# Recurrent block of a two-layer fp32 kernel: the Gelu branch with tokens on partitions, the first convolution tap on ScalarE, the end of the block in quarters

## Chip, cores, metric

One NeuronCore of a Trainium2 chip runs the whole program. The metric is device time in microseconds (us), the median of several executions. Engines are named as in the profile: PE (TensorE matmul), PEld (its weight load), DVE (VectorE), ACT (ScalarE), POOL (GpSimd), SP (SyncE, which issues the weight transfers).

## The reference, cut to the block that changes

The program computes an attention layer with an MLP, a recurrent layer with an MLP, and then a second network (convolution and linear-attention mixing, then a mixture of experts with gathered rows). Only the recurrent layer's mixer is touched. Its input h is 256 tokens by 1024 features, everything is fp32.

```python
def rglru_block(h, w_in, conv_w, conv_b, w_a, b_a, w_x, b_x, lam, w_o):
    proj = h @ w_in                                   # 1024 -> 2048
    gate = jax.nn.gelu(proj[..., :RG_WIDTH])          # RG_WIDTH = 1024
    xc = causal_depthwise_conv(proj[..., RG_WIDTH:], conv_w, conv_b)   # 4 taps
    xh = xc.reshape(B, S, RG_BLOCKS, RG_BLOCK_DIM)
    r = jax.nn.sigmoid(einsum('bshi,hij->bshj', xh, w_a) + b_a)
    i = jax.nn.sigmoid(einsum('bshi,hij->bshj', xh, w_x) + b_x)
    log_a = (-RG_C * r) * jax.nn.softplus(-lam)
    a = jnp.exp(log_a)
    bterm = jnp.sqrt(-jnp.expm1(2.0 * log_a)) * (i * xc)
    _, hs = lax.associative_scan(lru_combine, (a, bterm), axis=1)
    return (hs * gate) @ w_o
```

## The kernel before

Products in this part of the program are made exact to fp32 by splitting: each operand is held as a high part (fp32r) and a low part, and `products` (L2194) issues three matmuls, high by high, high by low, low by high (L2196, L2197, L2198). Weights come by DMA into a ring of four 1 MB slots (`wring`). Each slot is two units of 128x1024. ACT makes a unit's high part (`split_high`, L939, the copy in L947), DVE its low part (`split_low`, L1398, L1402). There are four buffers for split units, so ACT waits with unit n until PE has done the group that used unit n-4 (`used_at`). Both engines execute in program order, so the splits stand by hand between the other work of ACT and DVE.

PSUM has eight banks of 128x512. `Plan` gives each matmul group a bank and a number. PE opens a bank with `open_bank` (L2136), which waits until `bank_free` of that bank has counted every earlier use of it; the engine that reads a group out increments it. `across` (L2212) is the product with tokens on the output's partitions: for each half of 512 output columns it opens two banks (one for each 128 tokens, `ACROSS` names them) and runs over the units. For `rg_o` the banks are 4 and 5 for half 0, 6 and 7 for half 1.

The recurrent block runs thus (feature tiles m = 0..7 of 128 channels by 256 tokens, channels on partitions):

- PE computes rg0..rg7 (the convolution branch, columns 1024.. of `w_in`), each 24 matmuls of 256 columns (`project`, L2251), and after rg(m+2) the two gate products of tile m (`gate_inputs`, L2387), which need the convolved tile xc(m). Then rg8..rg15 (the Gelu branch), then 16 transposes of the `keyT` table (groups key0..key3 in banks 0 to 3, used much later), then `across("rg_o")`.
- DVE, in a loop over m: takes rg(m) out of PSUM with the norm factor (L1586), first tap with bias (L1588), three more taps (L1590), then one `split_low`. Then the products i*xc (L1596) with three splits, and the end: differences (L1604), products with the root (L1610), the scans (L1614), and between them the eight `gate_input` reads of the Gelu branch (L1580). Then the gated output in halves of 128x1024 (L1618), its low part (L1622, which increments `y_split`), three splits, four copies of the transposed keys out of PSUM (L1627), and `cross("rg_o")`.
- ACT, in a loop over m: one `split_high`, and from m = 3 on `decays(m-3)`: two sigmoids and a tanh (L1113, L1115, L1122). After the loop: split, decays(5), decays(6), split, decays(7), split, a table load (L1137), logarithms in halves (L1140, L1141) with a split after each half, then for each half the root (L1145) and four exponentials (L1147), a table load and eight Gelus (L1150), a split, the high part of the gated output in halves (L1155), two splits.

`link` makes DVE wait for its own instruction's end, `mark` does not. The split units are numbered here from the block's first (0 and 1 are rg0 and rg1, 8 to 15 the Gelu branch, 16 to 23 `rg_o`).

## Time and profile before

| | us |
|---|---|
| median of 3 runs | 1654.12 (1653.52 to 1655.22) |
| the profiled execution | 1647.37 |
| its span, first to last instruction | 1645.6 |
| PE busy / DVE busy / ACT busy | 1379.3 / 1065.1 / 561.6 |
| recurrent block, rg0 to the last `rg_o` matmul | about 337 to 427 of the span |

The profile gives each instruction's start and duration. "Idle before" is the time in which the engine waited, with the instruction or queue that ended it. Granted clock 1.00 is 2.4 GHz on TensorE, 0.50 is 1.2 GHz. The profiled execution ran 6.75 us under the median of the timed ones.

### The profile page before, as it was taken

How to read it: one execution, taken by the hardware profiler on the slowest of the kernel's cores; microseconds unless marked ns; L12 is line 12 of the kernel's file. 1: busy time of each engine (PE TensorE's matmuls, PEld its weight loads, DVE VectorE, ACT ScalarE, POOL GpSimd, SP SyncE). 2: the span in 40 equal slices, each digit the busy share in tenths (PEclk: the TensorE clock that was granted, in tenths of full speed). 3: DMA queues.
4: the chain of work that ended last, by engine and by line, in shares of the span. 5: the costliest groups of instructions: out<-in, count | busy, mean ns of one | idle time of the engine just before them, and what ended most of it. 6: DMA issues, size and time to landing. Idle time of an engine off the chain costs nothing.

```text
span 1645.6 us, 22695 instructions
## 1 busy us (share of the span) xinstructions
PE 1379.3 (84%) x8206; PEld 998.4 (61%) x8206; DVE 1065.1 (65%) x2068; ACT 561.6 (34%) x1048; POOL 533.2 (32%) x620
## 2 busy tenths in 40 slices
PE   8999999997999999999999729576776839776674
PEld 7888998897999888788888604222322314222231
DVE  4556774579776557977776957657584748655444
ACT  5545664457665443332441212111120211212111
POOL 8200001000000000000002656666756666666663
PEclk9999999998999999999999959788988969889897
DMA  7333656543565544312264989999999999999996
GB/s 250 127 128 115 193 183 214 185 138 128 176 189 196 194 163 128 103 54 79 78 227 173 393 333 355 367 369 403 358 337 376 370 360 374 378 362 367 372 385 257
DMA packets 184002, 408.96 MB, mean 249 GB/s; under 512 B 10658, under 2 KB 91852, under 8 KB 183900
## 3 DMA queue, kind: packets, MB, share of 16 engines
q0 software_dynamic: 74096, 269.52, 42.5%
q1 hardware_dynamic: 109500, 137.06, 25.8%
q8 instruction: 60, 0.98, 0.2%
q10 hardware_dynamic: 304, 1.05, 0.2%
q14 instruction: 42, 0.34, 0.1%
HBM read 406.54 MB, written 1.05 MB: 248 GB/s over the span
## 4 chain that ended last, share of the span: by engine, by line
PE 46%; issue 18%; POOL 17%; DVE 9%; another core or an unknown queue 6%; ACT 2%; DMA 1%; POOLq 0%; DVEq 0%; SPq 0%; ACTq 0%
PE banks L2196 11%; PE banks L2197 11%; PE banks L2198 11%; POOL arena L906 7%; POOL wring L906 5%; PE banks L2666 3%; PE banks L2431 3%; POOL h_raw L906 3%; PE banks L2528 1%; POOL sq L906 1%; PE banks L2422 1%; DVE w_a_low L1402 1%; DVE h_raw L1650 1%; DVE arena L1590 1%
## 5 line engine op out<-in xcount | busy, mean ns | idle before, releaser
L906 POOL DMA_INDIRECT arena<-in_expert_u_dram,eidx x117 | 110.6, 946 | 702.3 <-DVEq L2025 637.1
L1402 DVE TENSOR_TENSOR w_a_low<-wring,w_a_high 128x1024 fp32r<-128x1024 f32 x192 | 235.3, 1227 | 129.4 <-ACT w_a_high L947 124.7
L2703 PE MATMUL banks<-arena 128*128 128x512 f32 x416 | 210.0, 651 | 105.8 <-ACT arena L1366 57.1
L947 ACT ACTIVATE w_a_high<-wring 128x1024 fp32r<-128x1024 f32 x192 | 201.9, 1053 | 133.3 <-PE banks L2198 131.1
L1366 ACT ACTIVATE arena<-ident,arena 128x128 f32<-128x128 f32 x238 | 84.1, 395 | 461.2 <-remote 264.7
L2196 PE MATMUL banks<-h_high,w_a_high 128*128 128x256 f32 (+1 forms) x832 | 238.1, 286 | 0.9 <-DVE h_low L1424 0.6
L2197 PE MATMUL banks<-h_low,w_a_high 128*128 128x256 f32 (+1 forms) x832 | 235.0, 282 | 0.0
L2198 PE MATMUL banks<-h_high,w_a_low 128*128 128x256 f32 (+1 forms) x832 | 233.5, 281 | 0.0
L2703 PEld LDWEIGHTS banks<-arena 128*128 128x128 f32 x416 | 82.8, 207 | 230.2 <-issue 164.4
L2703 PE MATMUL banks<-wring,arena 128*128 128x512 f32 x308 | 150.6, 635 | 37.1 <-issue 32.1
L2045 DVE CUSTOM_DVE_ANT_0 arena<-arena,banks 128x1024 f32<-128x1024 f32 x117 | 142.8, 1221 | 48.3 <-issue 16.6
L2196 PEld LDWEIGHTS banks<-h_high,w_a_high 128*128 128x128 f32 x832 | 156.2, 188 | 3.1 <-DVE w_a_low L1402 1.0
L2198 PEld LDWEIGHTS banks<-h_high,w_a_low 128*128 128x128 f32 x832 | 157.3, 189 | 0.0
L2197 PEld LDWEIGHTS banks<-h_low,w_a_high 128*128 128x128 f32 x832 | 156.5, 188 | 0.4
L2703 PEld LDWEIGHTS banks<-wring,arena 128*128 128x128 f32 x308 | 59.6, 200 | 124.5 <-issue 119.3
L2045 DVE CUSTOM_DVE_ANT_0 arena<-wring,banks 128x1024 f32<-128x1024 f32 x77 | 94.0, 1221 | 46.7 <-DMA wring<-in_expert_u_dram,eidx 24.2
L906 POOL DMA_INDIRECT arena<-in_expert_v_dram,eidx x111 | 104.4, 940 | 39.4 <-issue 33.2
L2703 PE MATMUL banks<-h_raw,arena 128*128 128x512 f32 x152 | 76.6, 646 | 28.0 <-issue 26.5
L2196 PE MATMUL banks<-w_a_high,u_high 128*128 128x512 f32 x256 | 99.8, 390 | 0.0
L2198 PE MATMUL banks<-w_a_high,u_low 128*128 128x512 f32 x256 | 99.6, 389 | 0.0
L2197 PE MATMUL banks<-w_a_low,u_high 128*128 128x512 f32 x256 | 99.6, 389 | 0.0
L906 POOL DMA_INDIRECT wring<-in_expert_u_dram,eidx x77 | 72.5, 941 | 52.2 <-remote 27.4
(401 smaller groups left out, 2386.4 us busy)
## 6 DMA issues: line engine op xcount, KB each, us to landing
wring<-in_mlp_w_dram SPq DMA_DIRECT2D x64, 1024.0 KB, 5.4
wring<-in_w_in_dram SPq DMA_DIRECT2D x19, 1024.0 KB, 5.6
wring<-in_sb_w_qkv_dram SPq DMA_DIRECT2D x12, 1024.0 KB, 5.3
wring<-in_rg_w_in_dram SPq DMA_DIRECT2D x8, 1024.0 KB, 5.7
wring<-in_w_q_dram SPq DMA_DIRECT2D x8, 1024.0 KB, 5.3
wring<-in_sb_w_o_dram SPq DMA_DIRECT2D x4, 1024.0 KB, 5.3
wring<-in_rg_w_o_dram SPq DMA_DIRECT2D x4, 1024.0 KB, 5.0
wring<-in_w_o_dram SPq DMA_DIRECT2D x4, 1024.0 KB, 7.5
```

Source lines behind the costliest of these rows:

```text
L906: g.indirect_dma_start(out=grow(j), out_offset=None, in_=(expert_u, expert_v)[which][0], in_offset=bass.IndirectOffsetOnAxis(ap=eidx[:, tt ...
L947: a.activation(unit(n, 0), raw_unit(n), ACT.Copy).then_inc(w_high, 1)
L1366: a.activation(diag[:, n % DIAGS, :], ident[:], ACT.Copy, scale=coef[:, tt, c0 + r:c0 + r + 1]).then_inc(diag_ready, 1)
L1402: v.tensor_tensor(unit(n, 1), raw_unit(n), unit(n, 0).bitcast(F32), ALU.subtract).then_inc(w_split, 1)
L1590: link(v.scalar_tensor_tensor(xc[:, m, :], xraw[:, m, t:t + SEQ], pc(5 + t, m), xc[:, m, :], ALU.mult, ALU.add))
L2045: ins = v.tensor_tensor_reduce(out=junk, in0=grow(j), in1=f_bank[tt][:, :], scale=1.0, scalar=0.0, op0=ALU.mult, op1=ALU.add, accum_out=do ...
L2196: mm(dst, left[0], right[0], start=first, stop=False)
L2197: mm(dst, left[0], right[1], start=False, stop=False)
L2198: return mm(dst, left[1], right[0], start=False, stop=last_)
L2431: last = mm(pb[:, 0:SEQ], w[:, kt, P * (m % 2):P * (m % 2 + 1)], hT[:, kt, real], start=kt == 0, stop=kt == KT - 1)
L2666: last = mm(pb[:, 0:SEQ], w[:, kt, P * (j % 2):P * (j % 2 + 1)], hT[:, kt, real], start=kt == 0, stop=kt == KT - 1)
L2703: last = mm(y_banks[tt][half][:, :], diag[:, n % DIAGS, :], grow(j)[:, 512 * half:512 * (half + 1)], start=False, stop=True, skip_group_ch ...
```

## The change

The Gelu branch is no longer computed channel by channel. `across`-like groups `rg_gate` (two halves of 512 columns, each with two banks for 128 tokens each) put tokens on partitions; ACT applies the Gelu straight from PSUM with the token's norm factor as scale, in four instructions of 128x512. PE transposes the result back (groups G0..G3, four transposes each, banks 5, 6, 1, 2), alternating with key0..key3, which now go to banks 7, 0, 3, 4. DVE's eight `gate_input` reads are gone. The first convolution tap is an ACT Identity with scale and bias, between two waits (`raw_ready`, `tap_ready`). The products i*xc of tiles 0 to 3 move into DVE's loop. The gated output, its high part and its low part go in quarters of 128x512, G read from PSUM. The low parts, four weight splits and the four key copies stand in a new order on DVE. One ACT split moves from between the logarithms to behind the Gelus.

```diff
@@ -201,12 +201,17 @@
         plan.add(f"ri{m - 2}", 2 * m % BANKS)
-    for name, b in (("rg8", 0), ("ri6", 7), ("rg9", 1), ("ri7", 6)):
-        plan.add(name, b)
-    for m in range(KT + 2, 2 * KT):
-        plan.add(f"rg{m}", m - KT)
-    for m in range(4):
-        plan.add(f"key{m}", m)
+    for half in range(2):
+        for u in range(KT // 2 - 1):
+            plan.mark(f"rg_gate{half}_u{u}")
+            if half == 0 and u < 2:
+                plan.add(f"ri{KT - 2 + u}", 1 + u)
+        for tt in range(2):
+            plan.add(f"rg_gate{half}_{tt}", ACROSS["rg_gate"][2][2 * half + tt])
+    for half in range(2):
+        for j in (2 * half, 2 * half + 1):
+            plan.add(f"G{j}", (5, 6, 1, 2)[j])
+            plan.add(f"key{j}", (7, 0, 3, 4)[j])
     plan.across("rg_o")
@@ -355,7 +360,7 @@
 _at = 0
-for _name, _count in (("qkv", 12), ("wo", 4), ("up0", 16), ("down0", 16), ("rg_in", 8), ("rg_o", 4),
+for _name, _count in (("qkv", 12), ("wo", 4), ("up0", 16), ("down0", 16), ("rg_in", 4), ("rg_gate", 4), ("rg_o", 4),
                       ("up1", 16), ("down1", 16), ("w_conv", 4), ("w_rwkv", 7), ("w_gate", 8),
@@ -370,7 +375,7 @@
           "rg_o": (3, KT, (4, 5, 6, 7), (0, 1, 2, 3)), "down1": (4, FF // P, (0, 1, 2, 3), (4, 5, 6, 7)),
-          "wo2": (5, KT, (0, 1, 2, 3), (4, 5, 6, 7))}
+          "wo2": (5, KT, (0, 1, 2, 3), (4, 5, 6, 7)), "rg_gate": (0, KT, (7, 0, 3, 4), ())}
 CROSSED_BY = {b: name for name, (b, _, _, _) in ACROSS.items()}
...
@@ -534,10 +539,11 @@
         squ = area(SPLIT_END + 4 * SEQ, 4, SEQ)
-        gate = area(8192, KT, SEQ)
+        gate = area(8192, 2, D)
         xraw = area(10240, KT, SEQ + CONV - 1)
         xc = area(12312, KT, SEQ)
         rS, iS, aS, tS, mS = (area(14360 + 2048 * j, KT, SEQ) for j in range(5))
+        gy = iS
         bd = area(24600, 2, KT, P)
...
@@ -770,9 +776,8 @@
             load_mlp(0)
-            for j in range(8):
-                c0 = (D if j < 4 else 0) + 256 * (j % 4)
-                load(SLOTS["rg_in"] + j, rg_w_in[0].rearrange("(k p) n -> p k n", p=P)[:, :, c0:c0 + 256], KT, 256)
+            load_columns("rg_in", rg_w_in[0], D, 4)
+            load_across("rg_gate", rg_w_in[0])
             load_across("rg_o", rg_w_o[0])
@@ -1124,6 +1129,9 @@
             for m in range(KT):
+                act.wait_ge(raw_ready, m + 1)
+                a.activation(xc[:, m, :], xraw[:, m, 0:SEQ], ACT.Identity, scale=par[:, 5 * KT + m:5 * KT + m + 1],
+                             bias=par[:, 9 * KT + m:9 * KT + m + 1]).then_inc(tap_ready, 1)
                 split_high()
@@ -1139,20 +1147,23 @@
                 a.activation(tS[:, h4], tS[:, h4], ACT.Ln, bias=1.0).then_inc(at_ready, 1)
-                split_high()
+                if m == 0:
+                    split_high()
             for m, h4 in enumerate(halves):
                 act.wait_ge(m_ready, m + 1)
                 a.activation(mS[:, h4], mS[:, h4], ACT.Exp, scale=0.5).then_inc(mroot_ready, 1)
                 for k in range(h4.start, h4.stop):
                     a.activation(aS[:, k, :], rS[:, k, :], ACT.Exp, scale=lamc[:, 4, k:k + 1]).then_inc(at_ready, 1)
-            for m in range(KT):
-                act.wait_ge(gate_in, m + 1)
-                a.activation(gate[:, m, :], gate[:, m, :], ACT.Gelu_apprx_tanh).then_inc(gelu_done, 1)
+            for half in range(2):
+                for tt in range(2):
+                    pb = wait_group(act, f"rg_gate{half}_{tt}")
+                    a.activation(gate[:, tt, 512 * half:512 * (half + 1)], pb[:, :], ACT.Gelu_apprx_tanh,
+                                 scale=rr[:, 4 + tt:5 + tt]).then_inc(free(f"rg_gate{half}_{tt}"), 1)
             split_high()
-            for m in range(2):
-                act.wait_ge(y_ready, m + 1)
-                h4 = slice(4 * m, 4 * m + 4)
-                a.activation(m_hl[0][:, h4, :], gate[:, h4, :], ACT.Copy).then_inc(gate_high, 1)
+            for j in range(KT // 2):
+                act.wait_ge(y_ready, j + 1)
+                a.activation(m_hl[0][:, 2 * j:2 * j + 2, :], gy[:, 2 * j:2 * j + 2, :], ACT.Copy).then_inc(gate_high, 1)
+            split_high()
             split_high(2)
@@ -1573,59 +1584,76 @@
-            def gate_input(first, last_):
-
-                for k in range(first, last_):
-                    pb = wait_group(dve, f"rg{KT + k}")
-                    link(v.tensor_tensor(gate[:, k, :], pb[:, 0:SEQ], rs[:, 0:SEQ], ALU.mult))
-                    dve.sem_inc(free(f"rg{KT + k}"), 1)
-                    dve.sem_inc(gate_in, 1)
+            def input_gate(m):
+
+                wait_out(dve, f"ri{m}")
+                mark(v.scalar_tensor_tensor(iS[:, m, :], iS[:, m, :], 2.0 ** 0.5, xc[:, m, :], ALU.mult, ALU.mult))
             for m in range(KT):
                 pb = wait_group(dve, f"rg{m}")
                 link(v.tensor_tensor(xraw[:, m, CONV - 1:], pb[:, 0:SEQ], rs[:, 0:SEQ], ALU.mult))
                 dve.sem_inc(free(f"rg{m}"), 1)
-                link(v.tensor_scalar(xc[:, m, :], xraw[:, m, 0:SEQ], pc(5, m), pc(9, m), ALU.mult, ALU.add))
+                dve.sem_inc(raw_ready, 1)
+                if m >= 4:
+                    input_gate(m - 4)
+                dve.wait_ge(tap_ready, m + 1)
                 for t in range(1, CONV):
                     link(v.scalar_tensor_tensor(xc[:, m, :], xraw[:, m, t:t + SEQ], pc(5 + t, m),
                                                 xc[:, m, :], ALU.mult, ALU.add))
                 dve.sem_inc(xc_ready, 1)
                 split_low()
-            for m in range(KT):
-                wait_out(dve, f"ri{m}")
-                mark(v.scalar_tensor_tensor(iS[:, m, :], iS[:, m, :], 2.0 ** 0.5, xc[:, m, :], ALU.mult, ALU.mult))
-                if m >= 5:
+            for m in range(4, KT):
+                input_gate(m)
+                if m > 4:
                     split_low()
             settle()
-            gate_input(0, 3)
             halves = [slice(0, KT // 2), slice(KT // 2, KT)]
             for m, h4 in enumerate(halves):
                 dve.wait_ge(at_ready, KT + 2 * m + 2)
                 link(v.tensor_tensor(mS[:, h4], mS[:, h4], tS[:, h4], ALU.subtract))
                 dve.sem_inc(m_ready, 1)
-                gate_input(3 + m, 4 + m)
-                split_low()
+                if m == 0:
+                    split_low()
             for m, h4 in enumerate(halves):
                 dve.wait_ge(mroot_ready, m + 1)
                 link(v.tensor_tensor(iS[:, h4], iS[:, h4], mS[:, h4], ALU.mult))
-                gate_input(5 + m, 6 + 2 * m)
                 dve.wait_ge(at_ready, KT + 4 + 4 * (m + 1))
                 for k in range(h4.start, h4.stop):
                     mark(v.tensor_tensor_scan(rS[:, k, :], aS[:, k, :], iS[:, k, :], 0.0, ALU.mult, ALU.add))
                 settle()
-            for m, h4 in enumerate(halves):
-                dve.wait_ge(gelu_done, h4.stop)
-                v.tensor_tensor(gate[:, h4], gate[:, h4], rS[:, h4], ALU.mult).then_inc(y_ready, 1)
-            for m in range(2):
-                h4 = slice(4 * m, 4 * m + 4)
-                dve.wait_ge(gate_high, m + 1)
-                v.tensor_tensor(m_hl[1][:, h4], gate[:, h4], m_hl[0][:, h4].bitcast(F32),
+
+            def gated(j):
+
+                pb = wait_group(dve, f"G{j}")
+                two = slice(2 * j, 2 * j + 2)
+                v.tensor_tensor(gy[:, two, :], pb[:, :].rearrange("p (k n) -> p k n", n=SEQ), rS[:, two, :],
+                                ALU.mult).then_inc(y_ready, 1)
+
+            def gated_low(j):
+
+                dve.wait_ge(y_ready, j + 1)
+                dve.sem_inc(free(f"G{j}"), 1)
+                two = slice(2 * j, 2 * j + 2)
+                dve.wait_ge(gate_high, j + 1)
+                v.tensor_tensor(m_hl[1][:, two, :], gy[:, two, :], m_hl[0][:, two, :].bitcast(F32),
                                 ALU.subtract).then_inc(y_split, 1)
-            split_low(3)
+
+            gated(0)
+            gated(1)
+            split_low()
+            gated_low(0)
+            gated(2)
+            gated_low(1)
+            gated(3)
+            gated_low(2)
+            gated_low(3)
+            split_low()
             for m in range(4):
                 pb = wait_group(dve, f"key{m}")
                 v.tensor_copy(keyT[:, 4 * m:4 * m + 4, :].rearrange("p a n -> p (a n)"),
                               pb[:, :]).then_inc(free(f"key{m}"), 1)
+                if m < 2:
+                    split_low()
             cross("rg_o")
@@ -2394,17 +2422,36 @@
             spread("rb2", 4)
-            for m in range(2, 2 * KT):
+            for m in range(2, KT):
                 project([f"rg{m}"], "rg_in", h_real, first=m)
-                if m < KT + 2:
-                    gate_inputs(m - 2)
+                gate_inputs(m - 2)
+            for half in range(2):
+                pbs = [open_bank(f"rg_gate{half}_{tt}") for tt in range(2)]
+                for u in range(KT // 2):
+                    w = split_unit(UNIT["rg_gate"] + KT // 2 * half + u)
+                    for tt in range(2):
+                        for kt in (2 * u, 2 * u + 1):
+                            last = products(pbs[tt][:, :], [t[:, kt, META + tt * P:META + (tt + 1) * P] for t in h_hl],
+                                            [t[:, kt - 2 * u, :] for t in w], kt == 0, kt == KT - 1)
+                        if tt or u == KT // 2 - 1:
+                            last.then_inc(group_done, 1)
+                    if half == 0 and u < 2:
+                        gate_inputs(KT - 2 + u)
             pe.wait_ge(keys_loaded, 16)
-            for m in range(4):
-                pb = open_bank(f"key{m}")
-                for j in range(4):
-                    last = transposed(pb[:, j * P:(j + 1) * P], keyT[:, 4 * m + j, :], P)
-                last.then_inc(group_done, 1)
-            across("rg_o", m_hl, lambda kt: (y_split, kt // 4 + 1))
+            for half in range(2):
+                wait_out(pe, *[f"rg_gate{half}_{tt}" for tt in range(2)])
+                for m in (2 * half, 2 * half + 1):
+                    pb = open_bank(f"G{m}")
+                    for kt in (2 * m, 2 * m + 1):
+                        for tt in range(2):
+                            c0 = SEQ * (kt % 2) + tt * P
+                            last = transposed(pb[:, c0:c0 + P], gate[:, tt, kt * P:(kt + 1) * P], P)
+                    last.then_inc(group_done, 1)
+                    pb = open_bank(f"key{m}")
+                    for j in range(4):
+                        last = transposed(pb[:, j * P:(j + 1) * P], keyT[:, 4 * m + j, :], P)
+                    last.then_inc(group_done, 1)
+            across("rg_o", m_hl, lambda kt: (y_split, kt // 2 + 1))
             mlp(1)
@@ -2636,9 +2683,9 @@
                 whole_gate(m)
-            pe.wait_ge(y_split, 3)
+            pe.wait_ge(y_split, 5)
             project([f"yb{m}" for m in range(KT)], "rwkv_out", lambda kt: [y[:, kt, :] for y in y0_hl])
-            pe.wait_ge(y_split, 4)
+            pe.wait_ge(y_split, 6)
             project([f"ya{m}" for m in range(KT)], "conv_out", lambda kt: [y[:, kt, :] for y in y1_hl])
```

(In the hunks left out, `used_at` covers the new group names, the semaphores are renamed, and later waits on `y_split` count two more.)

## Rows read from the trace of the kernel before

**Rows 1.** Windows of the trace: span stretches, busy time of each engine, granted clock, DMA.

```profile
core 0: us, PE busy (x) PEld busy (x) DVE busy (x) ACT busy (x) POOL busy (x), PEclk, DMA share, GB/s
...
396.40:402.30 5.90, 0.00 (x0) 0.01 (x1) 5.87 (x8) 3.40 (x5) 0.00 (x0) 0.51 0.00 1
402.30:415.20 12.90, 12.88 (x48) 10.48 (x49) 10.37 (x12) 4.83 (x5) 0.00 (x0) 0.83 0.62 189
```

**Rows 2.** Timeline of PE, start of `rg_o`: start, duration, instruction, idle before it.

```profile
402.32 0.77 PE L2196 MATMUL banks<-w_a_high,m_high 128*128 128x512 f32 x1 [8.77 <-DVE m_low L1622]
```

**Rows 3.** Timeline of DVE: first round of the convolution loop, start of the last.

```profile
343.71 0.42 DVE L1586 TENSOR_TENSOR arena<-banks,rs 128x256 f32<-128x256 f32 x1
344.28 0.41 DVE L1588 TENSOR_SCALAR arena<-arena,par 128x256 f32<-128x256 f32 x1 [0.15 <-DVE arena L1586]
344.73 1.52 DVE L1590 SCALAR_TENSOR_TENSOR arena<-arena,par 128x256 f32<-128x256 f32 x3
346.40 1.23 DVE L1402 TENSOR_TENSOR w_a_low<-wring,w_a_high 128x1024 fp32r<-128x1024 f32 x1
...
370.89 0.42 DVE L1586 TENSOR_TENSOR arena<-banks,rs 128x256 f32<-128x256 f32 x1
```

**Rows 4.** Timeline of DVE: scans, gated output, splits, key copies.

```profile
391.07 2.44 DVE L1614 TENSOR_TENSOR_SCAN arena<-arena 128x256 f32<-128x256 f32 x4 [0.24 <-DVE arena L1580]
393.54 1.22 DVE L1610 TENSOR_TENSOR arena<-arena 128x1024 f32<-128x1024 f32 x1
...
395.47 0.42 DVE L1580 TENSOR_TENSOR arena<-banks,rs 128x256 f32<-128x256 f32 x1 [0.24 <-DVE arena L1580]
...
398.60 2.36 DVE L1618 TENSOR_TENSOR arena<-arena 128x1024 f32<-128x1024 f32 x2
...
403.23 3.49 DVE L1402 TENSOR_TENSOR w_a_low<-wring,w_a_high 128x1024 fp32r<-128x1024 f32 x3
406.64 2.47 DVE L1627 COPY arena<-banks 128x512 f32<-128x512 f32 x4
```

**Rows 5.** Timeline of ACT: the release of a Gelu by DVE's read of 395.47.

```profile
396.08 0.42 ACT L1150 ACTIVATE arena<-arena 128x256 f32<-128x256 f32 x1 [0.25 <-DVEq L1582]
```

**Rows 6.** Timeline of ACT, second network: four Identity with scale and bias.

```profile
654.83 2.18 ACT L1206 ACTIVATE arena<-arena,omka,par 128x288 f32<-128x288 f32 x4
```

**Rows 7.** Timeline of ACT: splits, decays, table load, logarithms, roots.

```profile
369.62 1.06 ACT L947 ACTIVATE w_a_high<-wring 128x1024 fp32r<-128x1024 f32 x1 [1.65 <-PE banks L2198]
370.58 0.46 ACT L1113 ACTIVATE arena<-banks,par 128x256 f32<-128x256 f32 x1
...
371.69 0.47 ACT L1113 ACTIVATE arena<-banks,par 128x256 f32<-128x256 f32 x1
...
377.64 1.06 ACT L947 ACTIVATE w_a_high<-wring 128x1024 fp32r<-128x1024 f32 x1 [1.67 <-PE banks L2198]
378.72 1.28 ACT L1137 ACT_TABLE_LOAD   x1
380.01 1.16 ACT L1140 ACTIVATE arena<-arena,eps 128x1024 f32<-128x1024 f32 x1
...
382.02 1.04 ACT L947 ACTIVATE w_a_high<-wring 128x1024 fp32r<-128x1024 f32 x1
382.97 1.14 ACT L1140 ACTIVATE arena<-arena,eps 128x1024 f32<-128x1024 f32 x1
...
388.45 1.05 ACT L1145 ACTIVATE arena<-arena 128x1024 f32<-128x1024 f32 x1
...
391.11 1.28 ACT L1150 ACT_TABLE_LOAD   x1
```

**Rows 8.** Groups by line, ACT from 402.3 on: a 128x512 instruction, busy, mean ns.

```profile
L994 ACT ACTIVATE sq<-xres 128x512 f32<-128x512 f32 x4 | 2.5, 629 | 2.3 <-DVEq L1442 2.3
```

**Rows 9.** Source line of the transposes, 388 to 420: ns min/median/max, first and last start.

```profile
L2145 PE MATMUL banks<-ident,arena x16: 270/272/273, 391.6 to 393.3; 128*128 128x128 f32 x16
```

**Rows 10.** Timeline of PE at the start of the program: 16 transposes.

```profile
5.38 3.67 PE L2145 MATMUL banks<-ident,xres 128*128 128x128 f32 x16 [2.60 <-DMA xres<-in_x_dram]
```

More of the change, by code:

```diff
@@ L403, in make_used_at @@
         of(name, *[f"{name}{half}_{f'u{u}' if u < last else 1}" for half in range(2) for u in range(last + 1)])
-    of("rg_in", *[f"rg{m}" for m in range(2 * KT)])
+    of("rg_in", *[f"rg{m}" for m in range(KT)])
     of("w_conv", *[f"{n}{m}" for n in ("val", "cg") for m in range(RT)])
@@ L625, in build @@
             "h_whole", "h_high", "w_high", "w_split", "gate_high", "y_high", "y_split", "mix_high"))
-        gate_in, gelu_done = sem("gate_in"), sem("gelu_done")
+        raw_ready, tap_ready = sem("raw_ready"), sem("tap_ready")
         mix_split, meta_ready, meta_high, meta_split = map(sem, (
```

## Prediction

> **What bounds the kernel now.** I read the windows first. PE works without a gap until 393.5, the end of the key transposes, and then stands: from 396.4 to 402.3 it is busy for 0.00 us while DVE is busy for 5.87 of 5.90 [rows 1]. The timeline names the wait: `rg_o` begins at 402.32 after 8.77 us of idling, released by DVE's first low part L1622 [rows 2]. So within the block the end of DVE's chain sets the time, and PE sets it again from 402.32 on. While PE stands its clock is granted at half (0.51, 1.2 GHz), and it is still at half when PE resumes: the stretch from 402.3 to 415.2, which is half 0 of `rg_o`, has a mean of 0.83, and 12.9 x 0.17 = 2.2 us are lost to it [rows 1]. A block that kept PE fed could give 8.8 + 2.2 = 11 us. The whole question is when `rg_o` can start. Ahead of that I follow three clocks: DVE's loop, ACT's order behind it, and DVE's last stretch.
>
> **Step 1, the convolution loop (longer).** In a round DVE starts its PSUM read at 343.71, the first tap at 344.28, the other taps at 344.73, so these begin 1.02 us behind the read, and the split follows at 346.40 [rows 3]. The change replaces DVE's tap of 0.41 us by a trip to ACT and back. The hand-over from a DVE read that counts a semaphore by hand to an ACT start is 0.61 us from the read's start: 395.47 to 396.08 [rows 4, 5]. The Identity itself: four with scale and bias on 288 columns took 2.18 us, one every 0.55 or less [rows 6]; I take 0.60 us from start to result for 256 columns and 0.50 until ACT's next instruction. With 0.03 back to DVE the taps begin 1.24 us behind the read, 0.22 later than now. If the Identity took 0.45 as ACT's sigmoids of this width do (0.46) [rows 7], it would be 0.07; if the way back cost 0.1 more, 0.32. So DVE does one instruction less in each round and the round still grows, by 0.22 (0.07 to 0.32): nothing is put in the hole in tiles 0 to 3, and in tiles 4 to 7 the product i*xc, another 256-wide instruction of 0.4 us, fits in it. The last round's read moves from 370.89 [rows 3] by 7 x 0.22 = 1.5 to 372.4, its tap on ACT starts at 373.0, and xc(7) is ready at about 375.1.
>
> PE follows this loop, since each pair of gate products waits for xc(m). Its Gelu units end by about when today's do (the transposes behind them begin at 391.6 [rows 9]; the loop gives up to 1.8 us, eight units less of small matmuls take some back), near 392, and the first Gelus come later than that, so nobody on the path waits for them.
>
> **Step 2, ACT falls behind (the largest term).** Today ACT's split of round m waits for PE's group rg(m), which is early; the split at 369.62 and decays(5), (6) at 370.58 and 371.69 are done before DVE has finished round 7 [rows 7]. In the changed program each round of ACT begins with a wait for DVE's read, and what is queued behind it waits too: the split, the decays, and after the last round everything to the table load. From the tap's 373.0: 0.50, split 0.96, decays(4) 1.11, split 0.96, decays(5) and (6) 2.22, split 0.96, decays(7) 1.11, split 1.08, which is 8.9 us, all in ACT's order, by the spacings 369.62, 370.58, 371.69 and 377.64, 378.72 [rows 7]. The table load starts at 381.9 and not at 378.72: 3.2 us later. Today the split at 377.64 waits for PE (1.67 us idle) [rows 7]; that slack is used up.
>
> From the logarithms at 380.01 to the load at 391.11 ACT takes 11.10 us, with two splits of 0.95 (382.02 to 382.97) [rows 7]. One of them moves behind the Gelus. So the first half's exponentials end at 388.45 - 0.95 + 3.2 = 390.7, the second half's at 391.11 - 0.95 + 3.2 = 393.4.
>
> DVE then: first scans from 390.8, 2.47 us (391.07 to 393.54); product with the root 1.24; second scans 2.47 [rows 4]. They end at 397.0. Today they end at 398.60. The eight `gate_input` reads and a split that stood between are gone, and of what that frees 1.6 us are left.
>
> The Gelus: load 1.3, then two 128x512 at 0.63 [rows 8], done at 395.9; G0 is ready at 396.6, ahead of DVE. Gelus three and four end near 397.1.
>
> **Step 3, the order at the end (the turn).** PE opens bank 4 for the first `rg_o` group before its first matmul. In the changed plan the last earlier use of bank 4 is key3, and key3 is freed by DVE's last key copy. Today the keys lie in banks 0 to 3 and their copies (406.64, four in 2.47 us) run while PE already multiplies [rows 2, 4]. So quarters of the gated output don't let PE begin; the whole DVE sequence does: four gated products, four low parts, four key copies, four splits. Prices: a 128x1024 product is 1.18 (2.36 for two), so 0.60 for 512; a copy 0.62; a split 1.16 (3.49 for three) [rows 4]. From 397.0: gated 0 and 1 to 398.3; split to 399.4; low 0, gated 2, low 1, gated 3, low 2 to 402.4; low 3 waits for ACT's high part of quarter 3 (gated 3 ends 401.8, hand-over 0.2, 0.63 [rows 8]) and ends at 403.3; the next split waits for ACT's, made behind that high part, and runs 403.6 to 404.8; copy, split, copy, split, copy, copy: 4 x 0.62 + 2 x 1.16 = 4.8, to 409.6. PE starts at 409.7, 7.4 us later than 402.32.
>
> From there the same 96 matmuls and 8 transposes follow. All four units of half 0 are split by then, as they were in time before. The clock falls again (PE has only transposes from about 392 on, then idles some 10 us); I take the same 2.2 us of loss, between 0 and 3.4. Removed from PE are 8 units of 24 matmuls of 256 columns for 8 of 12 of 512, and added are 16 transposes, both ahead of the wait, so worth nothing. SP's transfers wait for splits that come at most 2 us later, and each unit is used 5 us or more behind; nothing on POOL moves.
>
> **Bounds.** Loop 0.07 to 0.32 per round: -1.1 to +0.8. Twelve 512-wide operations at 0.55 to 0.68: -0.6 to +1.0. Transposes: 16 take 1.8 us at full clock [rows 9] and 3.67 at the start of the program [rows 10]. If the clock has fallen before 396, G1 comes at 399.1 and holds `gated(1)` by 1.4. The clock's loss itself: -2.2 to +1.2. Taken together, with not all at one end, the shift is 4.9 to 10.4 us.
>
> The row shows the transposes today at 270 ns each, before the fall. The Trainium skill (TensorE: Matmul & The Clock Gate, "Part 4: PE-mode transpose") says that transposes don't count as PE activity for the clock. By that rule the clock is half under the new transposes, and the time would be 1.4 us over the forecast, 1662.9; the trace of before, where nothing follows the transposes, can't tell. The case itself (half clock before G1 is done) I give 0.4 within the forecast, and its 1.4 us lie in the range.
>
> The table load is 1.28 us and the next instruction starts at once (378.72, 380.01), behind a split that ended at 378.70 [rows 7]. The Trainium skill (ScalarE: Activation LUTs, "What ACT_TABLE_LOAD costs") gives 2.66 us for a switch, with a drain of 1.38. By it the load in round 3 would push ACT's tap of round 4 by some 1.2 us, to 1662.7. The row decides for 1.28.
>
> **The sum.** The profiled execution took 1647.37; 7.4 more is 1654.8. The median of the timed runs lies 6.75 above that execution, and 1654.12 + 7.4 = 1661.5.
>
> **Rivals.**
> - *Early opening (faster).* PE begins when the first low part is there, 400.1. This needs key3's copy to be no condition, against the plan's bank numbers. Even so units 17, 18 and 19 come at 404.8, 406.6 and 408.4, so half 0 ends at 408.4 + 2.7 = 411.1, or 413.4 at half clock, against 415.2: 1650 to 1652.3, taken as 1651. It turns to this side when the last condition of the first matmul is met before 402.3. For it: DVE has less to do and the high and low parts come in pieces. Chance 0.10.
> - *ACT keeps up (slower, less).* If ACT's queue absorbs the taps, the logarithms start at 380.01 as today and the scans end at 393.8; with the same last stretch PE starts at 406.5: +4.2, 1658.3. Against it: 8.9 us stand behind the last tap. Chance 0.13.
> - *Identity and sigmoid in different table sets.* Then each of rounds 4 to 7 has one more load before its tap: 4 x 1.28 = 5.1, 1666.6. Against it: at 654.83 Identity follows sigmoids with no load [rows 6]. Chance 0.04.
> - *It does not do what it says.* The tap leaves DVE, but DVE stands for the same time. That is in the forecast.
>
> **How the numbers follow.** The forecast 1661.5 has 0.73, its own range 1659.0 to 1664.5. With "ACT keeps up" and the bounds 4.9 to 10.4 the range is 1656.8 to 1664.8; left out is the early opening and the double load. A measurement can tell about 0.2%, 3.3 us, from no change: slower means over 1657.4. Slower holds the forecast and most of the second rival, 0.82; same 0.08, from the lower ends of both; faster 0.10.
>
> **What would show it.** DVE's rounds at 4.05 us and not 3.83; ACT's table load behind decays(7) near 382; scans ending near 397; `rg_o`'s first matmul near 409.7, released by a DVE copy of line L1627's kind and not by a low part, with PE idle for about 10 us ahead of it. If PE starts right behind the first low part, step 3 is wrong; if the load is at 378.7, step 2 is; if the rounds stay at 3.83, step 1 is.

## The result and the profile after

| | before | after |
|---|---|---|
| median | 1654.12 us (1653.22 to 1657.23) | 1674.66 us (1669.32 to 1678.02) |
| profiled execution | 1647.37 | 1678.02 |
| its span | 1645.6 | 1676.2 |

The ratio is 1.0117 (95% interval 1.0094 to 1.0139): 20.5 us slower, where 7.4 were forecast. The two profiled executions are 30.7 us apart, since that of before is 6.75 us under its median and that of after 3.4 us over its own. So I read each stage by itself and don't divide up the 30.7.

First the block. Timeline of DVE after: a round of the loop, then scans to key copies.

```profile
343.16 0.42 DVE L1594 TENSOR_TENSOR arena<-banks,rs 128x256 f32<-128x256 f32 x1
344.49 1.53 DVE L1601 SCALAR_TENSOR_TENSOR arena<-arena,par 128x256 f32<-128x256 f32 x3 [0.90 <-ACT arena L1133]
346.16 1.23 DVE L1413 TENSOR_TENSOR w_a_low<-wring,w_a_high 128x1024 fp32r<-128x1024 f32 x1
347.30 0.42 DVE L1594 TENSOR_TENSOR arena<-banks,rs 128x256 f32<-128x256 f32 x1
...
393.86 2.44 DVE L1622 TENSOR_TENSOR_SCAN arena<-arena 128x256 f32<-128x256 f32 x4
396.47 0.69 DVE L1629 TENSOR_TENSOR arena<-banks,arena 128x512 f32<-128x512 f32 x1 [0.17 <-PE banks L2173]
398.10 0.69 DVE L1629 TENSOR_TENSOR arena<-banks,arena 128x512 f32<-128x512 f32 x1 [0.95 <-PE banks L2173]
398.71 1.21 DVE L1413 TENSOR_TENSOR w_a_low<-wring,w_a_high 128x1024 fp32r<-128x1024 f32 x1
399.84 0.68 DVE L1638 TENSOR_TENSOR m_low<-arena,m_high 128x512 fp32r<-128x512 f32 x1
...
405.12 0.68 DVE L1653 COPY arena<-banks 128x512 f32<-128x512 f32 x1
...
408.58 1.28 DVE L1653 COPY arena<-banks 128x512 f32<-128x512 f32 x2
```

ACT after: the Identity, and the first table load behind the last split.

```profile
343.85 0.60 ACT L1133 ACTIVATE arena<-arena,par 128x256 f32<-128x256 f32 x1 [1.04 <-DVEq L1596]
...
380.03 1.09 ACT L952 ACTIVATE w_a_high<-wring 128x1024 fp32r<-128x1024 f32 x1
381.14 1.28 ACT L1145 ACT_TABLE_LOAD   x1
```

PE after: the new transposes, and the start of `rg_o`.

```profile
395.40 5.35 PE L2173 MATMUL banks<-ident,arena 128*128 128x128 f32 x32 [3.00 <-ACT arena L1160]
409.92 0.80 PE L2224 MATMUL banks<-w_a_high,m_high 128*128 128x512 f32 x1 [9.17 <-DVE arena L1653]
```

These answer rows 2 to 7 and 9. A DVE round goes from read to read in 4.14 us (343.16 to 347.30) at first and in 4.05 from then on, and DVE stands 0.90 us in it for ACT's tap. The quarters' first low part is done at 400.5, but PE waits 9.17 us for line L1653, the key copy, and starts at 409.92. The windows show what the clock took:

```profile
402.30:409.90 7.60, 0.00 (x0) 0.00 (x0) 7.21 (x10) 3.47 (x4) 0.00 (x0) 0.73 0.44 136
409.90:416.00 6.10, 6.08 (x14) 4.85 (x15) 0.00 (x0) 0.50 (x1) 0.00 (x0) 0.50 0.55 174
416.00:435.40 19.40, 19.40 (x91) 16.07 (x90) 11.45 (x14) 9.72 (x15) 0.00 (x0) 1.00 0.41 120
```

The first 6.1 us of `rg_o` run at 1.2 GHz: 3.05 us lost, against 2.2 in [rows 1]. To compare blocks I count from the first transpose of the crossing into the recurrent layer (336.71 before, 336.18 after) to the first matmul of the second network's z groups (635.65, 644.09): 298.94 us before, 307.91 after. The block costs 9.0 us.

That leaves over half of the result. From that z matmul to the first gathering DMA it is 255.3 us before (to 891.0) and 264.0 after (to 908.1), 8.7 more, in a stage that the change doesn't touch. With the two instruction streams side by side the place is the small products of the linear attention. PE's timeline there, before and then after:

```profile
691.51 0.69 PE L2456 MATMUL banks<-arena 64*64 64x64 f32 x32 [2.65 <-DVE arena L1787]
...
702.78 3.40 PE L2456 MATMUL banks<-arena 64*32 64x32 f32 x208
706.11 3.72 PE L2431 MATMUL banks<-sq,wring 128*128 128x256 f32 x16
```

```profile
699.96 1.13 PE L2503 MATMUL banks<-arena 64*64 64x64 f32 x32 [2.66 <-DVE arena L1815]
701.02 6.46 PE L2469 MATMUL banks<-sq,wring 128*128 128x272 f32 x16
...
712.83 3.15 PE L2503 MATMUL banks<-arena 64*32 64x32 f32 x187
719.58 0.75 PE L2503 MATMUL banks<-arena 64*64 64x64 f32 x21 [3.60 <-issue]
720.26 5.17 PE L2478 MATMUL banks<-sq,wring 128*128 128x256 f32 x16
```

Before, 208 matmuls run in 3.40 us without a gap. After, PE stops behind the 187th for 3.60 us, and what it waits for is nothing that a semaphore shows ("issue"). The larger products ahead of the run and behind it take 6.46 us (at 701.02; 3.93 at full clock) and 5.17 us (3.72 before): the clock is at half there for a part of the time. Windows of after around the two places:

```profile
699.00:709.00 10.00, 9.04 (x129) 7.13 (x129) 9.51 (x20) 1.05 (x3) 0.00 (x0) 0.66 0.19 66
...
714.00:719.00 5.00, 1.97 (x133) 1.83 (x123) 0.35 (x1) 2.80 (x10) 0.00 (x0) 1.00 0.68 212
719.00:724.00 5.00, 4.42 (x32) 3.66 (x33) 0.00 (x0) 1.94 (x3) 0.00 (x0) 0.66 0.01 3
```

The page and the view of DMA have a queue that nobody in the kernel issues to. The first line stands in the page (the whole span), the second in the view of DMA for 716 to 719, in which one packet of 16 KB passes while PE stands:

```profile
q8 instruction: 60, 0.98, 0.2%
```

```profile
q8 instruction: 1, 0.02, 2.3%
```

I take this for PE's program being loaded, 60 packets of 16384 bytes. The idea to be tested: the change takes 80 matmuls with their 80 weight loads out of PE's program (the page counts 8206 matmuls before, 8126 after), with four further instructions 164 in all, so that every later block boundary falls 164 instructions further on in the work; two boundaries then fall into the 416 instructions (208 matmuls, 208 loads) that PE gets through in 3.4 us, and the second block isn't there in time.

### The profile page after: what moved, and what is told of

Its sections match the earlier page's. It is cut to its first block, busy times and chain, and to the rows that moved or that the text cites. A ratio compares the mean times of both kernels' runs of the same rounds, so it can differ in the third digit from the quotient of the medians.

```text
span 1676.2 us, 22521 instructions
## 1 busy us (share of the span) xinstructions
PE 1389.2 (83%) x8126; PEld 998.6 (60%) x8126; DVE 1060.0 (63%) x2056; ACT 563.6 (34%) x1054; POOL 533.3 (32%) x620
## 4 chain that ended last, share of the span: by engine, by line
PE 48%; issue 18%; DVE 14%; another core or an unknown queue 12%; POOL 4%; ACT 3%; DMA 1%; DVEq 0%; POOLq 0%; SPq 0%; ACTq 0%
PE banks L2224 11%; PE banks L2225 11%; PE banks L2226 11%; DVE arena L2073 3%; PE banks L2478 3%; PE banks L2713 2%; PE banks L2469 1%; PE banks L2575 1%; POOL arena L911 1%; POOL wring L911 1%; PE banks L2750 1%; PE banks L2173 1%; DVE h_raw L1678 1%; POOL h_raw L911 1%
## 5 line engine op out<-in xcount | busy, mean ns | idle before, releaser
L2224 PE MATMUL banks<-h_high,w_a_high 128*128 128x256 f32 (+1 forms) x768 | 219.5, 286 | 0.8 <-DVE h_low L1435 0.6
L2225 PE MATMUL banks<-h_low,w_a_high 128*128 128x256 f32 (+1 forms) x768 | 217.0, 283 | 0.0
L2226 PE MATMUL banks<-h_high,w_a_low 128*128 128x256 f32 (+1 forms) x768 | 215.5, 281 | 0.0
L2750 PE MATMUL banks<-wring,arena 128*128 128x512 f32 x308 | 156.8, 657 | 67.1 <-issue 51.0
L2224 PEld LDWEIGHTS banks<-h_high,w_a_high 128*128 128x128 f32 x768 | 144.1, 188 | 3.0 <-DVE w_a_low L1413 1.0
L2226 PEld LDWEIGHTS banks<-h_high,w_a_low 128*128 128x128 f32 x768 | 145.2, 189 | 0.0
L2225 PEld LDWEIGHTS banks<-h_low,w_a_high 128*128 128x128 f32 x768 | 144.4, 188 | 0.3
L911 POOL DMA_INDIRECT wring<-in_expert_v_dram,eidx x83 | 78.4, 945 | 32.1 <-issue 24.5
```

The costliest lines, as they stand in the source:

```text
L911: g.indirect_dma_start(out=grow(j), out_offset=None, in_=(expert_u, expert_v)[which][0], in_offset=bass.IndirectOffsetOnAxis(ap=eidx[:, tt ...
L2224: mm(dst, left[0], right[0], start=first, stop=False)
L2225: mm(dst, left[0], right[1], start=False, stop=False)
L2226: return mm(dst, left[1], right[0], start=False, stop=last_)
L2750: last = mm(y_banks[tt][half][:, :], diag[:, n % DIAGS, :], grow(j)[:, 512 * half:512 * (half + 1)], start=False, stop=True, skip_group_ch ...
```

## The experiments

The runs were made on several chips, and the kernel before takes 1654, 1649 or 1569 us on them, so only ratios to before on the same chip are compared, and stretches within the traces. "Stall" is the idle time ended by "issue" within the 208 products. The last column is the sum of PE's waits of that kind from the z group to the gather, the stall among them; one of 1.1 us, which comes last and is in all of the kernels, is left out.

| run | ratio (95%) | `rg_o` behind entry | entry to z | z to gather | stall | all such waits |
|---|---|---|---|---|---|---|
| before | 1 | 65.6 | 298.9 | 255.3 | none | 1.4 |
| after | 1.0117 (1.0094 to 1.0139) | 73.7 | 307.9 | 264.0 | 3.60 | 6.6 |
| after_b | 1.0111 (1.0091 to 1.0131) | 73.6 | 306.3 | 261.8 | 3.55 | 5.9 |
| b_pad92 | 1.0068 (1.0045 to 1.0091) | 69.1 | 302.2 | 263.5 | 3.60 | 7.4 |
| a_pad164 | 1.0123 (1.0068 to 1.0179) | 87.7 | 321.6 | 257.1 | none | 1.1 |
| a_fill41_b | 1.0064 (1.0048 to 1.0081) | 77.2 | 311.3 | 256.3 | none | 0.5 |
| a_fillmid | 1.0057 (1.0044 to 1.0071) | 73.8 | 308.0 | 255.2 | none | 1.1 |
| a_tapdve | 1.0079 (1.0055 to 1.0103) | 70.6 | 303.2 | 263.4 | 4.19 | 6.2 |
| a_banks | 1.0030 (1.0004 to 1.0057) | 64.3 | 297.4 | 262.6 | 3.92 | 5.9 |
| a_banks_fill41_b | 1.0021 (1.0011 to 1.0031) | 65.2 | 298.4 | 255.6 | none | 1.0 |
| best_b | 0.9988 (0.9978 to 0.9997) | 58.8 | 290.3 | 254.2 | none | 0.5 |
| best0 | 0.9996 (0.9986 to 1.0005) | 58.8 | 290.2 | 262.9 | 3.60 | 5.8 |
| best2 | 0.9943 (0.9929 to 0.9956) | 58.8 | 290.2 | 255.2 | none | 1.2 |

**Does the place of the blocks make the stall?** Into the kernel before, untouched otherwise, go 92 increments of a semaphore nobody reads: 92 more instructions, which with a block of 256 instructions puts the boundaries where 164 fewer put them.

```diff
+            for _ in range(92):
+                pe.sem_inc(pad, 1)
             across("rg_o", m_hl, lambda kt: (y_split, kt // 4 + 1))
```

> The kernel before with 92 such increments in PE's idle time ahead of rg_o: 92 is 256 minus 164, so the instruction blocks behind them lie as in the changed kernel, while nothing else moves. Theory A: PE stalls for about 3.6 us in the small products near 706 and the first gather comes up to 8 us later; about 1662. Rival B: no stall, within 0.2% of the kernel before, 1654.

PE's timeline in that run:

```profile
704.84 3.15 PE L2459 MATMUL banks<-arena 64*32 64x32 f32 x187
711.59 0.57 PE L2459 MATMUL banks<-arena 64*64 64x64 f32 x21 [3.60 <-issue]
```

The kernel before now has the stall of 3.60 us behind the same 187th matmul. None of the change is in it. Its page counts 61 packets on q8 and not 60. The increments aren't free: `rg_o` starts 3.5 us later behind the entry (69.1 for 65.6), and that is in the ratio too.

The reverse, 164 increments in the changed kernel at the same point:

> The changed kernel with 164 increments of an unused semaphore on PE, placed where PE idles ahead of rg_o. The change took 164 instructions (80 matmuls with their 80 weight loads, and 4 others) out of PE's program, so from there on its 16 KB instruction blocks lie on other code; 164 more put them back. Theory A (block placement): the 3.6 us stall of PE at 716 and the half-clock stretches at 699 and 720 go away, first gather issued about 9 us later than in the kernel before, not 17; time about 1665. Rival B (the later start of everything, in phase with the clock or the weight transfers, makes them): stall and half clock stay, about 1674. In both, rg_o starts as in the changed kernel, or up to 1 us later if an increment costs more than the 9 us of idle time divided by 164.

```profile
423.35 0.76 PE L2225 MATMUL banks<-w_a_high,m_high 128*128 128x512 f32 x1 [23.12 <-issue]
...
725.92 3.40 PE L2506 MATMUL banks<-arena 64*32 64x32 f32 x208
```

The stall is gone, 208 products in 3.40 us. But here PE sat 23.12 us before `rg_o`, up to 0.14 us for each increment, so the total says nothing. In the next runs 41 tiny products (four instructions each, their result unused) ahead of the transposes back take their place, and the changed kernel itself runs beside them:

```diff
+            for _ in range(41):
+                mm(bank[5][0:64, 0:32], ident[0:64, 0:64], ident[0:64, 0:32], start=True, stop=True)
```

> The changed kernel once more, as the yardstick for the others on this chip: about 1.2% over the kernel before; PE stalls for 3.6 us near 716; first gather issued 17 us later than before.

> The changed kernel with 41 tiny fp32 products (64x64 by 64x32, four PE instructions each, 164 in all) on a free bank where PE waits for the first Gelus. The semaphore increments of the earlier run cost 0.12 us each and delayed rg_o; these run at some 16 ns each, 1.4 us in a wait of 3 us. Theory A (block placement): rg_o starts as in the changed kernel (near 410), no stall in the small products, the clock stays up there, first gather 8 to 9 us after that of before instead of 17; time 8 us under the changed kernel. Rival B (lateness itself): stall stays, same time as the changed kernel.

```profile
391.77 6.47 PE L2442 MATMUL banks<-ident 64*64 64x32 f32 x82
398.18 5.37 PE L2173 MATMUL banks<-ident,arena 128*128 128x128 f32 x32
...
715.58 3.40 PE L2506 MATMUL banks<-arena 64*32 64x32 f32 x208
```

The ratio falls from 1.0111 to 1.0064 with the same 164 instructions back, though the products took 6.47 us, more than I had counted on, and put `rg_o` 3.6 us later. (The traced execution of a_fill41_b is the longest of its four, 5.7 us over their median.) A cheaper place was PE's wait of 2.66 us for DVE near 697, where the same 41 products, written in the small products' own form, took 1.51 us:

```diff
                 pairs([f"ntx_{tt}"], aa, kk, tt, swapped=True, pars=(1,))
+                if tt == 1:
+                    for i in range(41):
+                        h0 = HD * (i % 2)
+                        mm(bank[plan.at["ntx_1"][1]][h0:h0 + 32, 480:512], ident[h0:h0 + HD, h0:h0 + 32],
+                           ident[h0:h0 + HD, h0:h0 + 32], start=True, stop=True)
```

> The changed kernel, with 41 tiny products (64x32 by 64x32, into unused columns of a bank that is being written anyway; results not used) put where PE stands 2.66 us for DVE near 697 us. They add 164 instructions to PE's program, as many as the change took away, and touch nothing of the block. Theory 'placement of the instruction blocks': PE's stall of 3.6 us in the dense small products near 716 goes, and with it the dips of the clock; from the first z group to the first gather it takes 255 to 257 us, as in the kernel before, and not 262 to 264; rg_o still starts 7 to 8 us late. Ratio to before near 1.006. Rival 'what the changed block does later': the stall depends on what the block does (order of banks, DMAs), not on the count of instructions; then it stays, and the ratio is 1.011. A second rival: the 41 products cost as much as at their two earlier places, 5 to 6.5 us, only 2.7 of it hidden; then the ratio is 1.008.

```profile
697.07 1.51 PE L2533 MATMUL banks<-ident 64*32 64x32 f32 x82
699.79 0.69 PE L2503 MATMUL banks<-arena 64*64 64x64 f32 x32 [1.22 <-DVE arena L1815]
...
711.07 3.40 PE L2503 MATMUL banks<-arena 64*32 64x32 f32 x208
```

With `rg_o` as late as in after (73.8 us behind the entry), the stretch to the gather is that of before, and the ratio is 1.0057: 8.9 us on this chip. That is the price of the changed block, and it agrees with 308.0 - 298.9 = 9.1 us. The rest of the 20.5 lies behind the block.

**Where in its program does PE stand?** The traces hold a record for each matmul, weight load and semaphore instruction of PE, and they can be counted. Ahead of the stall stand 9481 records in after, after_b, a_tapdve, a_banks and best0, and 9737 in b_pad92, which is 256 more. Within 35 us after stands three more times with no releaser:

```profile
732.09 1.27 PE L2575 MATMUL banks<-arena 64*64 64x64 f32 x37 [0.66 <-issue]
741.63 1.39 PE L2575 MATMUL banks<-arena 64*64 64x64 f32 x51 [0.99 <-issue]
751.90 1.32 PE L2575 MATMUL banks<-arena 64*64 64x64 f32 x44 [1.31 <-issue]
```

Ahead of these stand 9993, 10505 and 11017 records: 9481 and 2, 4 and 6 times 256. All the waits in the table's last column, 36 in the thirteen traces, stand at 9481 records or a multiple of 256 away from it. So these waits mark the block boundaries. The 208 products begin behind record 9102 in the kernels with 164 fewer and behind 9266 in those without a stall: the former cross two boundaries in the run, behind 9225 and 9481, the latter only one, behind 9481. (In b_pad92 they begin behind 9358, and the two boundaries are 9481 and 9737.) After crosses the first at 713.85 and goes on behind the second at 719.58, 5.7 us later. In a_fillmid these two boundaries are passed 5.8 us apart (706.99 and 712.77) by the work alone, and nothing waits. Lateness isn't the cause: a_banks and best0 are early and have the stall, a_pad164 and a_fillmid are late and don't.

**Is it the order at the end?** Only the banks of `rg_o` are reordered, so that its first group doesn't need key3's bank:

```diff
-           "rg_o": (3, KT, (4, 5, 6, 7), (0, 1, 2, 3)),
+           "rg_o": (3, KT, (5, 6, 4, 7), (0, 1, 2, 3)),
```

> The changed kernel with rg_o's banks (5, 6, 4, 7) for (4, 5, 6, 7): half 0 no longer waits for the copy of key3, only for the low part of quarter 1. Theory of the last key copy: PE starts rg_o near 401.8 and not at 409.9, released by a low part, then waits for the splits of its units (404, 406, 408 on DVE's order), half 0 ends near 412 to 414 and not at 423; time 9 to 11 us under the changed kernel, 1664, if the later stall stays. Rival (the weight splits or the quarters set the start): rg_o starts later than 404 and the time is within 4 us of the changed kernel's.

```profile
400.76 0.47 PE L2224 MATMUL banks<-w_a_high,m_high 128*128 128x512 f32 x1
...
405.25 0.50 PE L2224 MATMUL banks<-w_a_high,m_high 128*128 128x512 f32 x1 [1.50 <-DVE w_a_low L1413]
```

`rg_o` starts right behind the transposes and the first low part; the next wait is for a split (1.50 us), which step 3's order put behind the quarters. The block falls from 9.0 us over before to 1.5 under it. Its stall (3.92 us) stays. Banks and fill together:

> The same filling and rg_o's banks (5, 6, 4, 7). Both causes gone: rg_o starts near 401 and waits for units' splits, block ends 1 to 2 us ahead of the kernel before, no stall; first gather within 2 us of before's; time from -3 to +1 us against the kernel before. If it stays 5 us or more over it, a third cause is open.

The stretches say 0.5 us less for the block and 0.2 more behind it; the ratio says 3.3 us more than before. On this chip the changed kernel too stands 3.6 us above what its stretches give (17.4 by the ratio, 7.4 + 6.5 by the stretches). Most of this goes with the traced execution: it lies 2.2 us under the median of its runs in a_banks_fill41_b and 2.7 in after_b, while the ratio goes by all of them. There is no trace of the kernel before from this chip, so where the last 1 to 1.5 us lie is open.

**Is it the tap?** The first tap goes back to DVE, with the product i*xc out of ACT's hole but still inside the loop:

```diff
-                act.wait_ge(raw_ready, m + 1)
-                a.activation(xc[:, m, :], xraw[:, m, 0:SEQ], ACT.Identity, scale=par[:, 5 * KT + m:5 * KT + m + 1],
-                             bias=par[:, 9 * KT + m:9 * KT + m + 1]).then_inc(tap_ready, 1)
...
-                dve.wait_ge(tap_ready, m + 1)
+                link(v.tensor_scalar(xc[:, m, :], xraw[:, m, 0:SEQ], pc(5, m), pc(9, m), ALU.mult, ALU.add))
```

> The changed kernel with the first tap back on DVE (one tensor_scalar, no waits between the engines); all else as changed. Theory of steps 1 and 2: ACT runs ahead again, its table load behind the splits comes near 379 and not 381.1, the scans end near 394 and not 396.3, rg_o starts 2 to 2.5 us earlier; rounds of 3.83 us for tiles 0 to 3 and 4.2 for 4 to 7, since the product has lost its hole. Time 2 us under the changed kernel. Rival (the tap on ACT costs nothing): same start of rg_o within 0.5 us.

```profile
393.76 3.68 PE L2169 MATMUL banks<-ident,arena 128*128 128x128 f32 x32 [1.50 <-ACT arena L1157]
407.11 0.79 PE L2220 MATMUL banks<-w_a_high,m_high 128*128 128x512 f32 x1 [9.67 <-DVE arena L1649]
```

The table load comes at 379.49, the scans end at 394.66 and `rg_o` starts at 407.11, released by the key copy again. So the tap on ACT costs 3.1 us of the 8.1 by which `rg_o` is late behind the entry (73.7 to 70.6). 2.0 of them are the scans, which end that much earlier. The other 1.1 are the transposes: they took 3.68 us at full clock behind a wait of 1.50 us, and 5.35 in after behind one of 3.00, and DVE's first two gated products didn't wait for them here. The 5.0 us that are left of the 8.1 still stand behind the key copy. The two prices overlap: a_banks, with the tap still on ACT, has `rg_o` 9.4 us earlier than after.

**A version that keeps the Gelu's part and drops the rest.** Tap and products back in DVE's order of before, banks 5, 6, 4, 7, each split of units 17 to 19 right behind a low part, key copies last, and one more of ACT's splits moved behind the first logarithms. Three forms: with the 41 products at the program's start, without them, and with them in the wait near 690.

```diff
             gated_low(1)
+            split_low()
             gated(3)
             gated_low(2)
+            split_low()
             gated_low(3)
```

> Built on the Gelu branch with tokens on partitions: first tap and products back on DVE as before, rg_o's banks (5, 6, 4, 7), DVE's splits of rg_o's units right behind the low parts and the key copies last, ACT's split of unit 14 behind the first logarithms, and the 41 tiny products at the start of the program. If the reading of the chains is right: ACT's table load near 376.5 and not 378.7, scans end near 392, rg_o starts near 396 within 2 us of the end of the transposes and the clock does not fall or falls for one short stretch; 6 to 9 us under the kernel before (0.4 to 0.5%). Rival (the splits or PE's own Gelu units bind instead): rg_o starts after 399, gain under 4 us.

> The fastest variant so far without its 41 tiny products at the start: first tap and products in DVE's loop as before the change, rg_o on banks 5, 6, 4, 7, splits 17 to 19 right behind the low parts, key copies last. Theory: the block gains 6 to 7 us against before (rg_o's first matmul near 394.7), the 4.5 us at the start are gone, and the stall of 3.6 us with its lower clock near 700 is back, +8 to +9: ratio near 1.001. Rival: the stall needs the exact length of the block as well, and does not come back here: ratio near 0.996.

> The same variant with the 41 tiny products put into PE's wait for DVE near 690 us instead of at the program's start. Theory 'placement': no stall, rg_o's first matmul near 394.7 against 402.3 before, nothing given back: 6 to 7 us under the kernel before, ratio 0.9955 to 0.9965. Rival 'the products cost 5 us wherever they are': ratio 0.998, as with the products at the start. Rival 'the gather stage at the end gives the time back': ratio over 0.998 though the stretch up to the first gather is 6 us shorter.

Timeline of PE of the last one, and its windows from 386 to 396 and on to 402:

```profile
391.17 3.66 PE L2164 MATMUL banks<-ident,arena 128*128 128x128 f32 x32
395.41 0.47 PE L2215 MATMUL banks<-w_a_high,m_high 128*128 128x512 f32 x1 [0.58 <-DVE m_low L1629]
...
694.00 3.40 PE L2494 MATMUL banks<-arena 64*32 64x32 f32 x208
```

```profile
386.00:396.00 10.00, 9.42 (x58) 8.00 (x58) 9.86 (x16) 9.21 (x15) 0.00 (x0) 1.00 0.27 103
396.00:402.00 6.00, 6.00 (x28) 4.95 (x27) 6.00 (x8) 4.79 (x6) 0.00 (x0) 1.00 0.54 164
```

PE stands 0.58 us before `rg_o` where it stood 8.77 [rows 2], and its clock is not lowered in the block. The block is 8.7 us shorter than before. Without the fill the stage with the stall takes 7.5 of that back (255.3 to 262.9) and nothing can be measured, 0.9996; with the fill at the start the products take 8.95 us and delay everything by 4.5; in PE's wait they cost nothing and the ratio is 0.9943, 8.9 us faster than before. The same edits are worth nothing or 0.6%, by the place of the block boundaries.

## Why the prediction was wrong

**What bounds, and step 1, were right.** 4.05 us a round, an Identity of 0.60 us, taps 1.33 behind the first read and then 1.24, as worked out from rows 3 to 6.

**Step 2 was right.** The load started at 381.14 for 381.9, the scans ended at 396.30 for 397.0; since the whole program stood 0.5 us earlier at the entry, the sizes agree within 0.3 us. a_tapdve shows that the tap was the cause: the load comes 2.0 us earlier behind the entry without it. *ACT keeps up* didn't happen, and from round 4 on no load stands between sigmoids and Identities. The one load in round 3 (357.58, 1.28 us) pushed no tap: the Identities around it start at 356.01 and 360.06, one round apart.

**Step 3 was right in kind and 0.9 us short.** `rg_o` started at 409.92, forecast 409.7, released by the key copy; a_banks shows that the bank was the cause. From the end of the scans to the first matmul it took 13.6 us, worked out 12.7. 0.95 of that is `gated(1)` waiting for the transposes, 5.35 us for 32, which ran at half clock until 398.95. I had carried this as a bound with chance 0.4 and 1.4 us. The Trainium skill (TensorE: Matmul & The Clock Gate, "Part 4: PE-mode transpose") has transposes not count as activity for the clock. The trace doesn't decide it: here PE had also stood idle for 3.00 us ahead of them. In best2, where they follow the products at once, all 32 ran at full clock (3.66 us), and so they did behind 1.50 us of idling in a_tapdve (3.68).

The term "clock loss" was 3.05 and not 2.2. Behind the entry `rg_o` starts 8.1 us late, and 8.1 + 0.85 is the 9.0 of the block, 1.6 over the 7.4 of the forecast and inside the bounds of 4.9 to 10.4. a_fillmid measures it alone, 1.0057. For *early opening* a_banks is the test: 1.5 us less than before by the stretches, at the weak end of the 1.8 to 4.1 given, because of the split that came late.

**The step that failed is one that I didn't write.** Of the matmuls removed from PE I said that they lie ahead of the wait and are "worth nothing", and that from `rg_o` on "the same" work follows. It does, but not from the same place in the program. b_pad92 gives the unchanged kernel the same stall, and a_pad164, a_fill41_b and a_fillmid take it away, each by a count of instructions alone; the stretch from z to the gather is 254.2 to 257.1 us in all runs with the boundaries as before, and 261.8 to 264.0 in all others. Against before that is 6 to 9 us, a term that the prediction put at nothing. The Trainium skill (Runtime: NRT & Kernel Launch, "Instruction fetch mechanics") says that the program comes in blocks of 16 KiB, 256 instructions, and that the cost of crossing one is "mostly hidden". The packets of 16384 bytes agree, and so do 164 + 92 = 256 and the steps of 256 records between the waits; "mostly hidden" holds for most of the 60 and not for four in after, at 3.6, 0.7, 1.0 and 1.3 us. In all thirteen traces the stall goes with two boundaries in the run of 208 products; why the second block comes no sooner isn't shown.

**Two things stay open.** Of the 8.7 us, 5.1 are waits for the program (6.6 us in all against 1.4 before): the stall of 3.6, and 1.5 more at the later boundaries. Most of the other 3.6 is clock at half, in two dips. The one behind the stall is 3.4 us long in after and 3.4 or 6.8 in the other five traces with a stall, and the traces without a stall don't have it. The other begins in PE's wait of 2.66 us for DVE near 699 and lasts 6.8 us. The kernel before, b_pad92 and best_b have the same wait (2.65 and 2.66) with no dip; a_pad164 and a_fill41_b have the dip of 6.8 us without any stall, and take 1.8 and 1.0 us more to the gather than before. So that dip doesn't come from the stall, and what decides it isn't settled; where the fill shortened the wait to 1.2 us there was none. And from the first gather to the end after's profile took 768.1 us, before's 754.7. In the traces of the other chips this stretch is the same within 5 us in changed and unchanged orders (752.2 to 757.1 on one, 677.2 to 679.7 on two), so I can't put it down to the change; the two traced executions alone lie 10.1 us further apart than the medians. The two stretches that are shown give 9.0 + 8.7 = 17.7 of the 20.5, and the other 2.8 stay open.

## What to carry to other kernels

When an edit changes how many instructions an engine has, look in the trace for the densest runs of small instructions behind it and for idle time there that no semaphore ends: an edit can be right and its gain go there, or a change that does nothing can look slow. Before judging such an edit, try it once with as many idle instructions put back, in a wait that is there anyway. And where work is cut into finer parts so that another engine can start sooner, follow the last condition of that engine's first instruction (here a bank), since the parts don't move it.

## What the runs showed of the hardware

- PE can stand 3.55 to 4.19 us for its own program, in 208 small products at 16 ns each, when two boundaries, 256 records apart, fall into them. In after one packet of the program passes within the stall.
- An increment of a semaphore on PE took up to 0.14 us (164 in 23.12 us), many times a small product with its weight load.
- 82 tiny matmuls took 1.51 us where successive ones used different halves of the rows, and 6.47 or 8.95 us where all used the same half and wrote to one place (64 columns of weights for 32, and the 6.47 in part at half clock); how much each of these does wasn't tried. The granted clock of the 8.95 us, at the program's start, can't be told from the rows, but the 16 transposes right behind took 3.68 us, about as long as 32 at full clock.
- 32 transposes of 128x128 took 3.66 us at full clock and 5.35 in a stretch that began at half.
